# Stacked high and low parts for the attention scores of the second layer of a two-block fp32 kernel

## What is computed

```python
def banded_attention(q, k, v, half_window, slopes, dist_scale, sink=None):
    ...
    s = jnp.einsum('nbqhgd,nbkhd->nbhgqk', qb, kw,
                   preferred_element_type=jnp.float32) * (dh ** -0.5) + bias
    s = jnp.where(mask[None, :, None, None], s, NEG)
    m = s.max(axis=-1)
    p = jnp.exp(s - m[..., None])
    l = p.sum(axis=-1)
    o = jnp.einsum('nbhgqk,nbkhd->nbqhgd', p, vw.astype(jnp.float32))
```

## Time and profile before

| | |
|---|---|
| median of 3 runs | 2562.41 us |
| the profiled execution | 2561.04 us, span 2559.3 us |
| TensorE matmul busy | 2519.4 us, 98% of the span |
| VectorE busy | 1977.7 us, 77% |
| ScalarE busy | 1072.1 us, 42% |
| GpSimd busy | 319.8 us, 12% |
| chain of work that ended last | TensorE 93%, VectorE 3%, ScalarE 2% |

### The profile page before, as it was taken

One profiled execution on the slowest core, in us unless ns is written; L12 is line 12 of the kernel. 1 busy time (PEld: TensorE's weight loads), 2 busy tenths in 40 slices (PEclk: granted clock), 3 DMA queues, 4 the chain that ended last, 5 costly groups with the idle time before them and its releaser, 6 DMA issues.

```text
span 2559.3 us, 37284 instructions
## 1 busy us (share of the span) xinstructions
PE 2519.4 (98%) x12662; PEld 2041.5 (80%) x12662; DVE 1977.7 (77%) x3476; ACT 1072.1 (42%) x2010; POOL 319.8 (12%) x454
## 2 busy tenths in 40 slices
PE   8999999999999999999999999999999999999998
PEld 6777688888888888777776888888888888878987
DVE  7899847889999898845555898988999987433566
ACT  6666815433333333455446453333334343111233
POOL 2011101000000000201111300000000017971000
PEclk9999999999999999999999999999999999999999
DMA  6334221221111211223232111111112132113122
GB/s 240 121 135 137 103 91 58 61 59 53 50 53 57 61 49 48 100 75 99 91 108 100 42 50 54 54 58 57 53 54 60 55 84 73 50 42 60 34 99 83
DMA packets 182018, 192.62 MB, mean 75 GB/s; under 512 B 18353, under 2 KB 146577, under 8 KB 181490
## 3 DMA queue, kind: packets, MB, share of 16 engines
q1 hardware_dynamic: 169954, 147.48, 18.1%
q0 software_dynamic: 11952, 43.65, 5.4%
HBM read 177.34 MB, written 12.58 MB: 74 GB/s over the span
## 4 chain that ended last, share of the span: by engine, by line
PE 93%; DVE 3%; ACT 2%; DMA 1%; issue 1%; POOL 0%; SPq 0%; DVEq 0%
PE psum L1438 21%; PE psum L1755 10%; PE psum L1757 10%; PE psum L1756 10%; PE psum L1807 4%; PE psum L1811 4%; PE psum L1808 4%; PE psum L1515 4%; PE psum L1517 4%; PE psum L1516 4%; PE psum L1796 3%; PE psum L1646 3%; PE psum L1630 2%; PE psum L1615 1%; DVE arena L2951 1%; PE psum L1611 1%
## 5 line engine op out<-in xcount | busy, mean ns | idle before, releaser
L3240 DVE SCALAR_TENSOR_TENSOR xT<-psum,mod,xT 128x512 f32<-128x512 f32 x504 | 356.4, 746 | 61.6 <-PE psum L1811 61.3
L2371 ACT ACTIVATE w_high<-wpair 128x512 fp32r<-128x512 f32 x240 | 146.5, 626 | 316.0 <-DVE wpair L3172 244.9
L1438 PE MATMUL psum<-hT_high,w_low 128*128 128x512 f32 x928 | 261.0, 392 | 0.2 <-DVE arena L2947 0.2
L1515 PE MATMUL psum<-hT_high,w_low 128*128 128x512 f32 x480 | 200.3, 417 | 5.0 <-DVE h_low_mix L3715 3.2
L1438 PEld LDWEIGHTS psum<-hT_high,w_low 128*128 128x128 f32 x928 | 173.0, 188 | 38.2 <-issue 2.5
L2589 ACT ACTIVATE arena<-arena 128x256 f32<-128x256 f32 (+3 forms) x296 | 146.6, 498 | 119.8 <-DVE arena L3526 119.6
L1517 PE MATMUL psum<-hT_high,w_low 128*128 128x512 f32 x480 | 189.1, 394 | 0.0
L1516 PE MATMUL psum<-h_low_mix,w_low 128*128 128x512 f32 x480 | 188.6, 393 | 0.0
L1757 PE MATMUL psum<-hT_high,w_low 128*128 128x512 f32 x480 | 186.7, 389 | 0.0
L1755 PE MATMUL psum<-hT_high,w_high 128*128 128x512 f32 x472 | 183.6, 389 | 0.0
L1756 PE MATMUL psum<-h_low,w_high 128*128 128x512 f32 x472 | 183.6, 389 | 0.0
(11 more groups left out here) (492 smaller groups left out, 6364.7 us busy)
## 6 DMA issues: line engine op xcount, KB each, us to landing
wpair<-in_ffn_w_in_dram SPq DMA_DIRECT2D x176, 256.0 KB, 2.9
wpair<-in_ada_tiles_dram POOLq DMA_DIRECT2D x20, 1024.0 KB, 5.2
arena<-in_ffn_w_out_dram SPq DMA_DIRECT2D x80, 256.0 KB, 2.9
wpair<-in_ada_tiles_dram POOLq DMA_DIRECT2D x32, 512.0 KB, 3.7
wpair<-in_w_in_dram SPq DMA_DIRECT2D x24, 512.0 KB, 3.8
wpair<-in_b_tiles_dram SPq DMA_DIRECT2D x18, 512.0 KB, 3.4
arena<-in_ada_tiles_dram SPq DMA_DIRECT2D x8, 1024.0 KB, 15.8
wpair<-in_a_tiles_dram SPq DMA_DIRECT2D x12, 512.0 KB, 5.1
```

The source lines that it names most:

```text
L1438: mm = nc.tensor.matmul(dst[:, HALF * a:HALF * a + HALF], w(k), src(k)[:, HALF * t:HALF * t + HALF], start=first and n == 0 and w is high ...
L1515: nc.tensor.matmul(dst, high[:, k, :], hT_high[:, k, rows], start=k == 0, stop=False)
L2371: nc.scalar.activation(of_step(s, first_high, part_high)[name], part_raw[name], ACT.Copy).then_inc(part_high_ready, 1)
L3240: nc.vector.scalar_tensor_tensor(xT[:, m, rows], psum[:, HALF * j:HALF * j + HALF], mod[:, l, 40 + m:41 + m], xT[:, m, rows], ALU.mult, AL ...
```

## The change

Layer two's scores are made as layer one's. `scores` has one form for all units: two fp32r matmuls per head over 128 rows, keys high and then low. `key_highs` and `query_highs` run for all units, and `queries` is gone; for layer two they write in the order of the dilation, and VectorE copies the values there (in layer one ScalarE does). `query_lows` runs for all units. The stacks lie in the arena, at other places than layer one's before. `k_ready` is gone.

Further edits: GpSimd makes the tables of unit u + 1 behind the first load of its group, not ahead of it. The first projections of units 1 and 5, and the turn of the values in units 0 and 4, wait for one release less. At the end of layer one, tile 22 is turned between the two score pairs of tile 24, and in both layers the second score pair of the last unit's tile 1 comes behind the turn and the outputs of that step. Tile 72 now scores its two pairs in the same two PSUM banks, and tile 73 waits accordingly.

```diff
@@ scores (TensorE)
-                    if a.layer == 1:
-                        pe.wait_ge(k_ready, 4 * (u - 3))
-                if n == ({1: 4, 2: 4, 3: 1}.get(u, 0) if pair == 1 else 0):
+                    pe.wait_ge(proj_free[1], bank_use(1, "q01", u) + 1)
+                if pair == 1 and n == {1: 4, 2: 4, 3: 1, 5: 4, 6: 1, 7: 1}.get(u, 0):
                     pe.wait_ge(proj_free[1], bank_use(1, f"q{pair}1", u) + 1)
...
-                    if a.layer == 0:
...
-                    rows = slice(DH * (h % 2), DH * (h % 2) + DH)
-                    nc.tensor.matmul(score_place(t, h)[:, lo:hi], lay["q"][rows, u % 2, h // 2, P * n:P * n + P],
-                                     lay["k"][rows, u % 2, key + lo:key + hi], start=True, stop=True).then_inc(scores_ready, 1)
+                    q, place, keys = q_tile(u, h, n), score_place(t, h)[:, lo:hi], slice(key + lo, key + hi)
+                    nc.tensor.matmul(place, q, k_high[a.layer][u % 2][:, keys], start=True, stop=False)
+                    nc.tensor.matmul(place, q, k_low[a.layer][u % 2][:, keys], start=False, stop=True).then_inc(scores_ready, 1)
@@ attention (TensorE)
-                    if t > 8 * first:
+                    if 8 * first < t < 8 * last - 9:
                         turn(t - 1)
                 for t in range(8 * last - 9, 8 * last + 2):
                     if t + 1 < 8 * last:
                         scores(t + 1, 0)
-                        scores(t + 1, 1)
+                        if first == 0 and t == 8 * last - 9:
+                            turn(t - 1)
+                        if t != 8 * last - 8:
+                            scores(t + 1, 1)
...
                     if t >= 8 * last - 8:
                         outputs(t - 2)
+                    if t == 8 * last - 8:
+                        scores(t + 1, 1)
@@ key_highs, query_highs (ScalarE)
+                for row in (0, DH):
+                    ins = nc.scalar.activation(k_half(k_high, u, half, slice(row, row + DH)), by_dilation(src[0:DH], a.dil), ACT.Copy)
...
+                for j in range(2):
+                    rows = slice(DH * j, DH * j + DH)
+                    ins = nc.scalar.activation(q_half(u, 2 * m + j, half, rows), by_dilation(src[rows], a.dil), ACT.Copy, scale=1 / 8)
+                ins.then_inc(q_high_ready, 1)
@@ attention (ScalarE)
-                    queries(first, 0, 0)
-                    tile_highs(("kv", first + 1))
-                    queries(first, 1, 0)
+                    key_highs(4, 0)
+                    query_highs(4, 0, 0)
+                    tile_highs(("kv", 5))
+                    query_highs(4, 1, 0)
...
-                    if u + 1 < min(last, 4) and n in (1, 3):
+                    if u + 1 < last and n in (1, 3):
                         key_highs(u + 1, n // 2)
@@ attention (VectorE)
+                for half in range(2):
+                    query_lows(first, 0, half)
                 values(first)
                 tile_lows(("kv", first + 1))
...
+                for half in range(2):
+                    query_lows(first, 1, half)
                 for t in range(8 * first, 8 * last + 3):
...
+                    if t in (64, 72):
+                        query_lows(u, 1, 1)
                     if t < 8 * last:
                         biased(t, 0)
...
+                    if first and u + 1 < last and n in (4, 6, 7):
+                        query_lows(u + 1, int(n == 7), int(n == 6))
@@ GpSimd
-                if u >= 1 and u + 1 < 4:
-                    bias_tables(u + 1)
                 for m in range(7 * u, min(7 * u + 7, 20)):
+                    if m == 7 * u + 1 and 1 <= u < 3:
+                        bias_tables(u + 1)
```

More of the change, by code:

```diff
@@ L361, in two_blocks_kernel @@
             extra = part("extra", [P, 3584])
+        with ExitStack() as parts:
+            part("before_arena", [P, 16 * S + 6144])
+            arena_part = part("arena_part", [P, 32256])
         hT = sb("hT", [P, KC, S])
@@ L1507, in project @@
                     if k == 0:
-                        pe.wait_ge(proj_free[half], bank_use(half, use, u))
+                        pe.wait_ge(proj_free[half], bank_use(half, use, u) - (1 if i == 0 and u in (1, 5) else 0))
                     project_chunk(u, what, half, k, psum[:, HALF * half:HALF * half + HALF])
@@ L2643, in attention @@
                         exponentials(t)
-                    if u < 3 and n == 5:
+                    if u + 1 < last and n == 5:
                         query_highs(u + 1, 0, 1)
@@ L2747, in _ @@
                 mix_shift(0, k)
+                if k == 2:
+                    key_highs(4, 1)
                 if k == 4:
[L2749 removed]
+                    query_highs(4, 0, 1)
                 if k == 6:
[L2751 removed]
+                    query_highs(4, 1, 1)
             attention(4, 10)
@@ L3473, in keys_values @@
                 src = psum[:, HALF * half:HALF * half + HALF]
-                if a.layer == 0:
-                    rows = slice(HALF * half, HALF * half + HALF)
-                    dve.wait_ge(k_high_ready, 2 * u + half + 1)
-                    for row in (0, DH):
-                        ins = nc.vector.tensor_tensor(k_low[u % 2][row:row + DH, rows], src[0:DH, :], as_f32(k_high[u % 2][0:DH, rows]), ALU.subtract)
-                    ins.then_inc(proj_free[half], 1)
-                    return
@@ new lines, in keys_values @@
+                high = as_f32(k_half(k_high, u, half, slice(0, DH)))
+                for row in (0, DH):
+                    ins = nc.vector.tensor_tensor(k_half(k_low, u, half, slice(row, row + DH)), by_dilation(src[0:DH], a.dil), high, ALU.subtract)
+                if a.layer == 1:
+                    dst = lay["vT"][0:DH, a.pad:a.pad + S]
+                    ins = nc.vector.tensor_copy(half_of(dst, half, a.dil), by_dilation(src[DH:P], a.dil))
+                ins.then_inc(proj_free[half], 1)
@@ new lines, in query_lows @@
+            def query_lows(u, m, half):
+                a = UNITS[u]
+                turn = 2 * m + half if u != 4 else (2, 0, 3, 1)[2 * m + half]
+                dve.wait_ge(q_high_ready, 4 * u + turn + 1)
+                src = psum[:, HALF * half:HALF * half + HALF] if u not in (0, 4) else first_place(f"q{m}", half)
+                for j in range(2):
+                    mine, other = slice(DH * j, DH * j + DH), slice(DH - DH * j, P - DH * j)
+                    ins = nc.vector.scalar_tensor_tensor(q_half(u, 2 * m + j, half, other), by_dilation(src[mine], a.dil), 1 / 8,
+                                                         as_f32(q_half(u, 2 * m + j, half, mine)), ALU.mult, ALU.subtract)
+                ins.then_inc(proj_free[half], 1)
@@ L3588, in attention @@
                         normalised(t - 1)
-                    if u + 1 < min(last, 4) and n in (4, 6, 7):
+                    if first == 0 and u + 1 < last and n in (4, 6, 7):
                         query_lows(u + 1, int(n == 7), int(n == 6))
@@ L3613, in attention @@
                         keep_spread(5)
-                    if t in (8, 16, 24):
+                    if first and u + 1 < last and n in (4, 6, 7):
+                        query_lows(u + 1, int(n == 7), int(n == 6))
+                    if first < u < min(last, 8) and n == 0:
                         query_lows(u, 1, 1)
```

85 lines of the change are left out of this document (35 added, 50 removed).

## The result

The changed kernel takes 2573.9 us in the median of six runs (2570.85 to 2577.77); the kernel before, in the runs beside it, 2562.73 (2561.18 to 2565.99). The ratio is 1.0044, 95% interval 1.0035 to 1.0054: about 11 us slower. The profiled execution of the change took 2577.77 us, span 2576.0, and is the longest of its six; against the one before it (2561.04) it is 16.7 us longer. So what follows is not a matter of the profiled execution alone, though a mean does not say where the clock was low.

What follows compares the result with a forecast made beforehand. TensorE was taken to bound layer two beside projections, ScalarE the last unit. Edits −2.0 − 0.2 − 2.0, scores +0.4, hand-overs +1.7 + 2.5 + 0.5 + 2.0 gave +2.9: median 2565 us, range 2554 to 2576.

Steps and rivals of the forecast that it cites:

- The price of a narrow stacked product: Layer two's scores on TensorE: 0.117 us per fp32r matmul at all three widths, a floor; sum +0.4 us.
- the rival without floor or waits: Narrow matmuls cost their columns, −7 us on scores, or hand-overs of 6.7 hide behind projections: 2556 us; chance 0.18.
- The rival of slow narrow fp32r: Below 256 columns fp32r runs at full fp32's rate: some +36 us, about 2601 us; chance 0.16.
- that of bare weight loads: Each change of weights costs 0.112 us on top of the columns: +43 us, 2608 us; chance 0.02.
- the row of one-column matmuls: Trace row of 32 one-column matmuls, 0.112 us each, read as weight loading and a floor under any width.
- Start of layer two: Second query pair's low parts on VectorE delay the first bias and second score pair: +1.7 us, bounds 0 and 3.4.
- Second tile of units 4 to 8: Keys' high parts on ScalarE delay the turned copy that TensorE's outputs read: +2.5 us for five units.
- Tile 64: Late query piece's high and low parts go ahead of the first bias, projections cover most: +0.5 us.
- The other edits: GpSimd tables behind a load −2.0, first projection of unit 1 −0.2, end of layer one −2.0 us.
- the first projection: Unit 1's first projection may begin sooner, but its scores wait for tile 0's bias: −0.2 us, between 0 and −0.5.
- Tile 72: Late query parts, uncovered, delay the first exponential in a unit bound by ScalarE: +2.0 us; shared-bank wait falls into that delay.
- The rival of larger hand-overs: One tile more per unit waits for the 1.3 us of a pair of low or high parts: 2571 us; chance 0.15.

Runs made afterwards that it cites:

- e1_busy72: The changed kernel with 24 products of 128 columns put into TensorE's idle time in tile 72; 2572.27 us, ratio 1.0032.
- e5_busy512: The changed kernel with 11 products of 512 columns put into TensorE's idle time in tile 72; 2572.37 us, ratio 1.0027.
- e9_busy512_rows: The changed kernel with 11 products of 512 columns in tile 72, VectorE's memset and row-sum copies moved from tile 73 to 72's start; 2567.26 us, ratio 1.0015.
- e8_fill72: The changed kernel with tile 71's turn and tile 70's outputs in tile 72's gap, first biases of tiles 64 and 72 before low parts; 2570.84 us.
- e7_unit9_old: The changed kernel with unit 9 scored as before in full fp32, the other units stacked; 2567.8 us, ratio 1.0014.
- e10_unit9_rows: The changed kernel with unit 9 scored as before, VectorE's memset and copies at the start of tile 72 instead of 73; 2564.87 us, ratio 1.0003.
- e6_wide_tail: The changed kernel with 11 products of 512 columns in tile 72 and one more ahead of each later score pair of unit 9; 2576.55 us, ratio 1.0047.
- e11_repaired: The changed kernel with keys' high parts behind exponentials, early biases, own work and 11 512-column products in tile 72's gap, early row-sum copies; 2564.32 us, ratio 1.0003.

## Why the prediction was right and where it was wrong

The range (2554 to 2576) held the time; the point, 2565, missed it by 9 us, and the likeliest class, no change, was wrong: it is slower. That the range held is luck: the forecast's own range ended at 2570, the rest up to 2576 was there for rivals, and neither the forecast nor a rival had what lengthened the kernel.

- *The price of a narrow stacked product* was right as a floor: 0.12 at 256 columns, 0.11 at 192 and 128 (0.117 was taken). The tiles measured −0.13, +0.02 and +0.19 against −0.13, +0.09 and +0.29; the first tiles of units 5 to 7, whose pairs lie apart, lost 0.49 to 0.50 each, and not 0.3. With the three delays below taken off (1.5, 3.3 and 0.6 us), some −1.1 us of layer two's +4.3 is left for the scores, where +0.4 was forecast. (Two slips in the sum change little: outside the first and second tiles there are 10 tiles of 256 columns and not 11, and the rival without floor or waits comes to 2558 by either of its terms, not 2556.) The rival of slow narrow fp32r and that of bare weight loads are both excluded by these rows; the row of one-column matmuls was the one to go by.
- *Start of layer two*: the first bias came at 1090.19, 4.55 us behind the first score in place of 0.67, and tile 34 lies 1.5 us later against the first score than before; +1.7 was forecast. TensorE's two waits there are 0.97 us, for the weights' low part, and 1.16, for the bias; the forecast had only the second.
- *Second tile of units 4 to 8*: +2.5 forecast, 3.3 measured by taking the cause away. TensorE waits 0.70 us at 256 columns, 0.59 at 192 and 0.39 at 128, where the estimates were 0.75, 0.45 and 0.1: the shorter exponentials shrank the wait, but less than supposed.
- *Tile 64*: +0.6 (3.30 us from its first pair to its second in place of 2.69), +0.5 forecast.
- *The other edits*: −4.2 forecast, −3.7 in the run with them alone, −4.2 in the trace. By parts the trace has −2.5 at tiles 9 and 17 (−2.0 forecast), nothing at the first projection (−0.2) and −1.7 at the end (−2.0): the sum agrees better than its terms. VectorE's wait for the load in tile 9 fell from 1.66 to 0.35 us, and TensorE's wait of the earlier trace rows is gone; the exponentials of the earlier trace rows came at 273.14 with 0.32 us of waiting.
- *Tile 72* is the step that failed. "+2.0" measured 12.9 in the profiled execution. Two things were wrong in it. The second pair does not "fall into the same delay": the first exponential came behind all four biases, and the second pair's came 1.15 us behind the first's, so that the exponential stood 4.76 us behind the tile's first score and not 3.9. Of this 0.9 about half is the order and half the clock: where the clock was still 1.00 (e1_busy72, e5_busy512, e9_busy512_rows) it stood 4.30 us behind. At full clock, with both holes closed, the tail is 3.1 us longer. And the text read the unit as bound by ScalarE and left the clock at 1.00: it had no term for what a longer idle time on TensorE does to the clock. That goes with the remainder, 9.8 us in the profile. The slow copies are a rival for part of it, and how much they add is open; but in e8_fill72, where they ran beside no subtraction (0.19 us each), 17 us of half clock still came with a tail of 33.8 us, 5.6 over that at full clock.
- *The rival of larger hand-overs* gave 2571, near the time but by another mechanism: in layer two up to tile 72 TensorE waits over 0.3 us only at the places named above.

A row for the clock was there, though not in the last unit of the kernel before, where the clock is 1.00 with waits of up to 1.12 us. It lies at the end of layer one, in the other unit without projections, beside the wait of the earlier trace rows. TensorE stood idle for 2.00 us, and the clock lay at half from 273.8 to 277.2 (TensorE's row, then windows):

```profile
272.83 0.44 PE L1611 MATMUL psum<-w_high,extra 128*128 128x384 f32 x1 [2.00 <-DVE extra L3494]
```

```profile
271.00:272.00 1.00, 0.00 (x0) 0.00 (x0) 0.97 (x3) 1.00 (x5) 0.00 (x0) 1.00 0.99 397
275.00:276.00 1.00, 1.00 (x6) 0.48 (x6) 0.96 (x7) 0.56 (x1) 0.20 (x1) 0.50 1.04 422
278.00:279.00 1.00, 1.00 (x7) 1.00 (x6) 0.78 (x4) 1.00 (x3) 0.00 (x0) 1.00 1.02 406
```

The edits left waits of 1.31 and 0.65 us there and, in the profile of the change, a clock of 1.00; so some of the −1.7 at this end may be the clock's. In e7_unit9_old the same 1.31 us was followed by half clock from 269.2 to 272.6, and layer one took 244.1 us in place of 242.4. The same wait thus came with a fall in one execution and without one in another: these traces give no length of wait that decides.

Shown by runs, in one profile each: that the clock falls behind idle time in tile 72 (also in the kernel before), that with wide products in the gap it stayed at 1.00 there and with narrow ones fell, that a second hole appears behind the slow copies, and that with both closed it stays. Not shown: how much of the change's own median the second matters for; there the clock was low already, and the four copies took 1.37 us beside GpSimd. Open, too, is why in e10_unit9_rows waits of 0.62 and 0.46 us came with a fall.

## What to carry to other kernels

Before moving work ahead of a wait on TensorE's last, uncovered unit, look for what TensorE does in that time: here an idle time of 2.74 us, priced at 2 us on the path, came with 24 us of half clock and a tail 12.9 us longer, and a stage bound by ScalarE turned into one bound by TensorE. Price a new idle time in a stream that had none with the stage at both levels of the clock, and look at the clock of the kernel's other uncovered stretches for a row. And where an engine's copies are shifted in time, look which instruction of GpSimd they now stand beside.

## What the runs showed of the hardware

- TensorE's clock fell from 2.4 to 1.2 GHz after a stretch in which it hardly waited: 24 products of 128 columns in 2.84 us, 0.39 us the longest wait, then the fall at 1377.6. After 11 products of 512 columns in that gap it did not fall there, in the profiles of four versions (e5_busy512, e6_wide_tail, e9_busy512_rows, e11_repaired).
- A VectorE copy within SBUF of 128 x 64 elements takes 0.19 us alone and took 2.33 and 2.35 us when a subtraction of GpSimd (2.35 us) had begun less than 0.1 us before it; the two ended within 0.1 us. A copy that had begun 0.06 us ahead of the subtraction took its usual 0.19. The Trainium skill ("SBUF — State Buffer", section "SBUF: two separate sides") says that the two engines share a pair of ports which, for some of VectorE's instructions, one holds for a whole instruction while the other blocks. The traces agree with that: in the changed kernel VectorE's bias instructions that read PSUM took their usual 0.29 us beside the subtraction.
- At half clock two neighbouring 128-column stacked products stand 0.21 to 0.22 us apart, at full clock 0.11: the floor goes with TensorE's clock. At half clock, in the changed kernel:

```profile
1378.49 0.41 PE L1634 MATMUL psum<-arena_part 128*128 128x128 f32 x1
1378.70 0.41 PE L1633 MATMUL psum<-arena_part 128*128 128x128 f32 x1
1378.92 0.41 PE L1634 MATMUL psum<-arena_part 128*128 128x128 f32 x1
```
